# Three pairs of modulation chunks loaded and multiplied at the second mixer's entry, with other router, gather and gate rows

## The reference

```python
def moe(h, router_w, router_b, w_up, b_up, w_down, b_down):
    logits = (xt @ router_w + router_b).astype(jnp.float32)
    top_vals, top_idx = lax.top_k(logits, TOP_K)
    gates = jax.nn.softmax(top_vals, axis=-1)
    ...  # each token's four experts: swiglu(x @ w_up[e] + b_up[e]) @ w_down[e] + b_down[e]
    contrib = y_slots[dest] * gate_sorted[:, None]
...
def second_block(x, c, ...):
    c_act = jax.nn.silu(c)
    for l in range(DEPTH):
        mod = c_act @ w_ada[l] + b_ada[l]
        sh1, sc1, g1, sh2, sc2, g2 = jnp.split(mod[:, None, :], 6, axis=-1)
        h = ada_norm(x, norm1_g[l], sh1, sc1)      # rms_norm(x, g) * (1 + scale) + shift
        proj = h @ w_in[l]
        ...  # neighbourhood attention, latent attention, short convolution, group norm: mixed
        x = x + g1 * (mixed @ w_out[l])
        h2 = ada_norm(x, norm2_g[l], sh2, sc2)
        gt, up = jnp.split(h2 @ w_gu[l], 2, axis=-1)
        x = x + g2 * ((jax.nn.silu(gt) * up) @ w_down[l])
```

## Time and profile before

| | us |
|---|---|
| median of three runs | 1532.1 (1530.83 to 1532.83) |
| profiled execution, own time | 1531.5 |
| its span, first to last instruction | 1529.6 |
| first mixer ends, branches begin | 201.2 |
| first expert product | 267.8 |
| second mixer begins | 1184.2 |
| TensorE busy | 1423.6 (93%) |
| VectorE, ScalarE, GpSimd busy | 591.9, 444.9, 39.1 |

### The profile page before, as it was taken

One profiled execution on the slowest core, in us unless ns is written; L12 is line 12 of the kernel. 1 busy time (PEld: TensorE's weight loads), 2 busy tenths in 40 slices (PEclk: granted clock), 3 DMA queues, 4 the chain that ended last, 5 costly groups with the idle time before them and its releaser, 6 DMA issues. The chain is left out here.

```text
span 1529.6 us, 19821 instructions
## 1 busy us (share of the span) xinstructions
PE 1423.6 (93%) x7981; PEld 838.8 (55%) x7981; DVE 591.9 (39%) x1030; ACT 444.9 (29%) x577; POOL 39.1 (3%) x80
## 2 busy tenths in 40 slices
PE   8999999999999999988988988989988999899998
PEld 8988798344334434323423423323333788788887
DVE  4985447211210211210210210210211786677765
ACT  5654533121111112111111111111111536454343
POOL 2000030000000000000000000000000022000000
PEclk9999999999999999999999999999999999999999
DMA  9598999899999999999999999999999361345552
GB/s 283 171 299 272 327 334 397 361 426 429 427 428 428 428 428 428 429 428 428 429 428 429 428 429 428 429 428 429 428 427 382 104 191 56 99 150 193 192 187 88
DMA packets 126901, 516.46 MB, mean 338 GB/s; under 512 B 6869, under 2 KB 95294, under 8 KB 102238
## 3 DMA queue, kind: packets, MB, share of 16 engines
q1 hardware_dynamic: 126558, 514.64, 84.6%
q10 hardware_dynamic: 288, 1.05, 0.2%
HBM read 514.62 MB, written 1.05 MB: 337 GB/s over the span
## 5 line engine op out<-in xcount | busy, mean ns | idle before, releaser
L1307 PE MATMUL ps<-ring,xg 128*64 128x512 f32 x1456 | 324.8, 595 | 27.3 <-DMA ring<-in_expert_w_up 23.2
L1450 DVE TENSOR_TENSOR glu<-ps,bupT 128x512 f32<-128x512 f32 x32 | 22.1, 692 | 717.5 <-PE ps L1316 717.5
L1307 PEld LDWEIGHTS ps<-ring,xg 128*64 128x64 f32 x1456 | 101.7, 137 | 244.8 <-issue 186.2
L86 ACT ACTIVATE hrow<-ps 128x1024 f32<-128x1024 f32 x32 | 32.7, 1023 | 474.4 <-PE ps L1307 474.4
L1332 PE MATMUL ps<-ring,act 128*64 128x512 f32 x608 | 136.8, 597 | 1.2 <-ACT y L86 1.1
L2134 PE MATMUL ps<-h_halves,w_hi 128*128 128x512 f32 x352 | 123.1, 394 | 1.1 <-DVE h_halves L2287 1.1
L2236 DVE TENSOR_TENSOR w_lo<-ring,w_hi 128x2048 fp32r<-128x2048 f32 x36 | 82.5, 2291 | 61.2 <-ACT w_hi L86 61.2
L1307 PE MATMUL ps<-more,xg 128*64 128x512 f32 x416 | 93.1, 595 | 8.4 <-DMA more<-in_expert_w_up 7.2
L2136 PE MATMUL ps<-h_halves,w_lo 128*128 128x256 f32 x352 | 98.7, 280 | 0.0
L86 ACT ACTIVATE y<-ps 64x512 f32<-64x512 f32 x64 | 37.8, 591 | 182.8 <-PE ps L1332 182.5
L86 ACT ACTIVATE w_hi<-ring 128x2048 fp32r<-128x2048 f32 (+1 forms) x38 | 70.7, 1864 | 60.0 <-PE ps L2136 32.6
(11 more groups left out here) (409 smaller groups left out, 2218.1 us busy)
## 6 DMA issues: line engine op xcount, KB each, us to landing
ring<-in_expert_w_up SPq DMA_DIRECT2D x91, 2048.0 KB, 36.8
ring<-in_expert_w_down SPq DMA_DIRECT2D x38, 2048.0 KB, 39.3
more<-in_expert_w_up SPq DMA_DIRECT2D x26, 2048.0 KB, 35.5
more<-in_expert_w_down SPq DMA_DIRECT2D x16, 2048.0 KB, 38.8
ring<-in_w_in SPq DMA_DIRECT2D x29, 1024.0 KB, 9.0
ring<-in_w_ada SPq DMA_DIRECT2D x24, 1024.0 KB, 6.5
x_xT_xn<-in_expert_w_up SPq DMA_DIRECT2D x11, 2048.0 KB, 36.9
ring<-in_w_gu SPq DMA_DIRECT2D x22, 1024.0 KB, 5.1
```

The lines of the kernel that those rows point to most:

```text
L86: return nc.scalar.activation(out, x, ACT.Copy)
L1307: last = nc.tensor.matmul(up[a2 * CAP:(a2 + 1) * CAP, u, :], k.xg[:, q, h * CAP:(h + 1) * CAP], w[:, c:c + 512], start=(q == 0), stop=(q = ...
L1450: link(nc.vector.tensor_tensor(k.glu[:, :, :, :], g, b[:, 0].to_broadcast(wide), ALU.add))
```

## The change

- Modulation pairs 7, 8 and 9 (shift and scale of the second norm, SHIFT2 and SCALE2, and the rows between, which nothing needs before the output block) leave the first mixer. The other nine run after chunks 6, 8, 9, 11, 12, 14, 15, 17 and 18.
- SyncE loads their six chunks at the end of the experts into ring slots 4, 5, 6, 2, 3 and 1, after w_in_2 chunk 0 and before chunks 1 to 4.
- TensorE multiplies them at the second mixer's entry, two pairs before the transposes and one behind, in place of `fill`; the sums are copied by ScalarE, turned by TensorE after projection 1, added to `k.mod` by VectorE, and GpSimd makes the second norm's scale from them.
- `PLACE_SLOT` has the slots of places 1 and 2 exchanged.
- The router: the second token tile's transposes go to two banks each, ScalarE copies one half and VectorE the other; logits are computed in pairs of tiles; the top four are found by replacing them in a copy and comparing; the place counts from 1, so a subtraction goes; the ungated `choose` is one compare instead of four.
- The gather is done in halves with a copy each; of the first expert pair's, four of eight tiles stand before the block's barrier.
- The gate row g1 is multiplied in two pieces between the logits; g2 is multiplied at the output block's entry and copied there.

```diff
-PLACE_SLOT = {0: 6, 1: 0, 2: 2, 3: 8, 4: 10, 6: 4}
+PLACE_SLOT = {0: 6, 1: 2, 2: 0, 3: 8, 4: 10, 6: 4}
...
-ADA_FROM = 8
+ADA_LATE = (7, 8, 9)
+ADA_AT = dict(zip((6, 8, 9, 11, 12, 14, 15, 17, 18), (a for a in range(N_ADA) if a not in ADA_LATE)))
+ADA_ORDER = list(ADA_AT.values())
+LATE_SLOTS = ((4, 5), (2, 6), (1, 3))
...
-        pair = i - 1 - ADA_FROM
-        if 0 <= pair < N_ADA:
+        pair = ADA_AT.get(i - 1)
+        if pair is not None:
             two = [("ada", 2 * pair), ("ada", 2 * pair + 1)]
             out += two if len(out) % RING1 < RING1 - 1 else two[::-1]
...
+    ada_products(nc, k, 7, k.cwin, pair, slots, pair == ADA_ORDER[0], pair == ADA_ORDER[-1])
+
+
+def ada_products(nc, k, bank, cwin, pair, slots, first, last_pair):
...
     w = k.ring[:, slots[0]:slots[1] + 1:slots[1] - slots[0], :].rearrange("p s (k n) -> p s k n", k=KD)
     for q in range(KD):
         g = 32 * (q % 4)
-        last = nc.tensor.matmul(k.ps[g:g + 32, 7, :].rearrange("p (s n) -> p s n", s=2),
-                                k.cwin[:, q, 31 - pair:63 - pair], w[:, :, q, :], start=(pair == 0 and q < 4),
-                                stop=(pair == N_ADA - 1 and q >= 4), skip_group_check=True)
+        last = nc.tensor.matmul(k.ps[g:g + 32, bank, :].rearrange("p (s n) -> p s n", s=2),
+                                cwin[:, q, 31 - pair:63 - pair], w[:, :, q, :], start=(first and q < 4),
+                                stop=(last_pair and q >= 4), skip_group_check=True)
     last.then_inc(k.ada_step, 1)
...
+    if not gated:
+        both = [P, TT, 2, CAP]
+        return nc.vector.tensor_tensor(k.sel.rearrange("p t (h n) -> p t h n", h=2),
+                                       k.slots[:, :].unsqueeze(1).unsqueeze(1).to_broadcast(both),
+                                       k.place[:, :, bass.ds(p * 2, 2)].unsqueeze(3).to_broadcast(both), ALU.is_equal)
...
-                    last = nc.tensor.transpose(k.ps[:, bank[t][half], j * P:(j + 1) * P],
+                    b, at = (bank[t][half], j) if t == 0 else (bank[t][half] + 4 * (j // 2), j % 2)
+                    last = nc.tensor.transpose(k.ps[:, b, at * P:(at + 1) * P],
...
-            def logits(t):
-                for half in range(2):
-                    if (t, half) == (1, 1):
-                        pe.wait_ge(hT_last, 1)
+            def logits(t, pairs):
+                for n in pairs:
+                    if t == 0:
+                        pe.wait_ge(hT_ready, n // 2 + 1)
                     else:
-                        pe.wait_ge(hT_ready, 2 * t + half + 1)
-                    for q in range(4 * half, 4 * half + 4):
+                        pe.wait_ge((hT_ready, hT_last)[n % 2], (3, 1)[n % 2] + n // 2)
+                    for q in (2 * n, 2 * n + 1):
                         last = nc.tensor.matmul(k.ps[:, 4 + t, 0:E], hT[:, q, t * P:(t + 1) * P], k.rw[:, q, :],
                                                 start=(q == 0), stop=(q == KD - 1))
...
+                return last
...
+            def gate_row(half):
+                return nc.tensor.matmul(k.ps[:, half, :], k.ones[:, :], k.diag[0][:, half * 512:(half + 1) * 512],
+                                        start=True, stop=True)
...
-            logits(0)
-            gate_rows(0)
+            logits(0, range(4)).then_inc(log_done, 1)
+            gate_row(0)
             turn(1, 0)
+            logits(1, (0,))
             turn(1, 1)
-            logits(1)
-            gate_rows(1)
+            logits(1, (1, 2, 3)).then_inc(log_done, 1)
+            gate_row(1).then_inc(gb_done, 1)
             pe.wait_ge(m_ready, 2)
...
-            fill(nc, k, 3, k.h[:, 0, 0:512], 1)
+            pe.wait_ge(k.hot_ready, 1)
+            gather(nc, k, 5, range(4)).then_inc(k.g_done, 1)
 
...
-                link(nc.vector.tensor_tensor(lg[:, t, :], k.ps[:, 4 + t, 0:E], k.rb[:, :], ALU.add))
+                link(nc.vector.tensor_tensor(lg[:, t, 0:E], k.ps[:, 4 + t, 0:E], k.rb[:, :], ALU.add))
                 link(nc.vector.max(m8[:, t, :], lg[:, t, :]))
-                nc.vector.tensor_scalar(k.small[:, t:t + 1], m8[:, t, 0:1], -1.0, None, ALU.mult).then_inc(negmax, 1)
-                link(nc.vector.max_index(ix[:, t, :], m8[:, t, :], lg[:, t, :]))
-                link(nc.vector.tensor_copy(ixf[:, t, :], ix[:, t, :]))
-                link(nc.vector.tensor_tensor(one_hot[:, t], bc(k.iota[:, 0:E], 1, 4), bc(ixf[:, t, 0:4], 2, E), ALU.is_equal))
-                nc.vector.tensor_reduce(k.chosen[:, t, :], one_hot[:, t].rearrange("p j e -> p e j"), AX.X, ALU.add)\
+                link(nc.vector.match_replace(rest_lg[:, t, :], m8[:, t, :], lg[:, t, :], -LARGE))
+                nc.vector.tensor_tensor(k.chosen[:, t, :], rest_lg[:, t, 0:E], lg[:, t, 0:E], ALU.not_equal)\
                     .then_inc(m_ready, 1)
+                nc.vector.tensor_scalar(k.small[:, t:t + 1], m8[:, t, 4:5], -1.0, None, ALU.mult).then_inc(negmax, 1)
 
...
-            for i, slot in enumerate(LATE):
+            def load_slot(i):
                 src, kt, cols = k.last[i]
-                sp.wait_ge(used, done + slot_free(slot))
+                sp.wait_ge(used, done + slot_free(LATE[i]))
                 sp.dma_start(slot_last(k, i, kt, cols), src).then_inc(k.last_in[i], 16)
+
+            load_slot(0)
+            for n, (pair, slots) in enumerate(zip(ADA_LATE, LATE_SLOTS)):
+                for c, slot in sorted(enumerate(slots), key=lambda x: slot_free(x[1])):
+                    sp.wait_ge(used, done + slot_free(slot))
+                    sp.dma_start(k.ring[:, slot, :].rearrange("p (k n) -> p k n", k=KD), k.ada_chunks[2 * pair + c])\
+                        .then_inc(k.first_in[n], 16)
+            for i in range(1, len(LATE)):
+                load_slot(i)
 
...
-            pe.wait_ge(hot_ready, 1)
-            gather(nc, k, 5, range(KD)).then_inc(g_done, 1)
+            gather(nc, k, 5, range(4, KD)).then_inc(g_done, 1)
             extra = extra_rounds(pe)
             pe.wait_ge(k.bias_in, 32)
             def up_weights(r, turn, at, n, h):
                 for q in range(KD):
+                    if h == 0 and q % 4 == 0:
+                        pe.wait_ge(xg_ready, n * 2 + q // 4 + 1)
                     if q % 2 == 0:
                         chunk = expert_arrived(k, pe, r, turn, at * PAIR + h * UP_CHUNKS + q // 2)
...
-            act.wait_ge(g_done, 1)
-            act_copy(nc, k.xg[:, :, :].rearrange("p k n -> p (k n)"), flat(rows)).then_inc(xg_ready, 1)
+            def gathered(n, src):
+                for half in range(2):
+                    act.wait_ge(g_done, n * 2 + half + 1)
+                    act_copy(nc, k.xg[:, 4 * half:4 * half + 4, :].rearrange("p k n -> p (k n)"), src[:, half, :])\
+                        .then_inc(xg_ready, 1)
+
+            gathered(0, rows)
...
+            def late_rows(n):
+                pe.wait_ge(k.first_in[n], 16 * (FIRST_LOADS[n] + 2))
+                ada_products(nc, k, 3, k.late_cwin, ADA_LATE[n], LATE_SLOTS[n], n == 0, n == len(ADA_LATE) - 1)
+
             pe.wait_ge(k.bm_in, 16 * len(k.bm_loads))
             for b in range(4):
-                nc.tensor.matmul(k.ps[:, b, :], k.flip[:, :], bias_window(k, b // 2, b % 2),
+                nc.tensor.matmul(k.ps[:, 4 + b, :], k.flip[:, :], bias_window(k, b // 2, b % 2),
                                  start=True, stop=True).then_inc(bm_done, 1)
-            fill(nc, k, 4, k.gB[:, 0, 0:512], 5)
-            for t in range(TT):
+            pe.wait_ge(k.ada_copied, 2)
+            for n in range(2):
+                late_rows(n)
+            for t in range(TT):
+                pe.wait_ge(bm_out, t + 1)
                 pe.wait_ge(xn_ready, t + 1)
                 for m in range(KD):
                     last = nc.tensor.transpose(k.flat[:, 2048 + t * D + m * P:2048 + t * D + (m + 1) * P],
                                                xn[:, t, m * P:(m + 1) * P], k.ident[:, :])
                 last.then_inc(xnT_done, 1)
-            pe.wait_ge(bm_out, 2)
-            fill(nc, k, 3, k.gB[:, 0, 0:512], 2)
-            pe.wait_ge(hT_ready, 3 + 2 * TT)
+            late_rows(2)
+            pe.wait_ge(hT_ready, 4 + 2 * TT)
             projection(0)
             for i in range(1, 4):
                 split_projection(i)
+                if i == 1:
+                    ada_turn(nc, k, pe, 3, k.late_acc, 7)
             half_projection(4, 0)
             pe.wait_ge(ck_n, 1)
             transpose_tokens(nc, k, k.flat[:, 2048:3328], proj[:, :, 768:1408], 0, 5).then_inc(ck_t, 1)
...
+            act.wait_ge(k.ada_step, N_ADA)
+            act_copy(nc, k.late_acc, k.ps[:, 3, :]).then_inc(k.ada_copied, 1)
...
+            dve.wait_ge(k.ada_summed, 2)
+            a0 = ADA_LATE[0]
+            v = k.mod[:, 4 * a0:4 * (a0 + len(ADA_LATE))].rearrange("p (a m) -> p m a", m=4)
+            nc.vector.tensor_tensor(v, v, k.ps[:, 7, 0:P].rearrange("p (m a) -> p m a", m=4)[:, :, a0:a0 + len(ADA_LATE)],
```

(20 more changed lines are left out.)

121 lines of the change are left out of this document (63 added, 58 removed).

## The result

The changed kernel takes 1552.6 us (median of 4 runs, 1551.95 to 1553.21) against 1532.5 (1530.83 to 1533.4), a ratio of 1.0129, 95% interval 1.0115 to 1.0143. It is slower, as forecast, but by 20.1 us and not 11.9, and 1552.6 lies outside the range of 1536 to 1549.

What follows compares the result with a forecast made beforehand. TensorE was taken to bound the first mixer and transfers the experts, with SyncE last at the barrier. 1531.5 - 7.3 - 0.1 + 18.0 + 0.1 + 0.8 + 1.0 = 1544.0 us, range 1536 to 1549.

Steps and rivals of the forecast that it cites:

- First mixer: TensorE-bound first mixer: nine modulation pairs instead of twelve and shorter waits save 7.3 us (bounds -5.0 to -8.9).
- I take 0.5 us of it: First mixer: 0.5 us saved of TensorE's 1.4 us wait for VectorE, bounds -1.0 and +1.4.
- a pair now runs one place earlier, which gives it time: First mixer: an earlier pair gives VectorE time, though TensorE's earlier arrival could keep or lengthen its 1.4 us wait.
- Router and bias: Experts' start: token tiles some 2 us earlier, but the down-projection bias transfer hides it; -0.1 us, bounds 0 and -2.0.
- The clock at the barrier: Behind the experts' barrier: a slower pace after TensorE idles some 18 us, +1.0 us, bounds 0 and +3.7.
- End of the experts: SyncE's six added w_ada chunks, 3.0 us each and uncovered, hold the barrier: +18.0 us, bounds +15 and +19.
- Second mixer: Second mixer: third pair's products in place of a fill +0.1 us, turn of the sums among dense projections +0.8 us.
- The rivals: Six chunks hidden (1525, 8 in 100); mixer transfer-held (1533.3, 5); router's 2 us real (1542, 10); costlier restart (1547, 12).
- The third: Router's 2 us are real because the bias lands earlier or is not waited for: 1542 us, 10 in 100.

Runs made afterwards that it cites:

- p_place: Changed kernel with its nine first-mixer pairs behind chunks 8 to 16 instead of 6 to 18: 1550.8 us, ratio 1.0116.
- p_router: The change without its modulation part (all twelve pairs in the first mixer; new router, gather and gate rows): 1535.9 us, ratio 1.0022.
- p_after_pad: Changed kernel with an unused 64-byte tile ahead of x_hi and x_lo, putting them 32 beyond a multiple of 256: 1550.7 us, ratio 1.0115.
- p_router_bias: The change without its modulation part, with TensorE's wait for the down biases moved to the first scatter: 1533.8 us, ratio 1.0000.
- p_warm20: Changed kernel with nineteen unread products behind TensorE's last scatter of the experts: 1551.0 us, ratio 1.0115.
- p_warm: Changed kernel with forty unread products behind TensorE's last scatter of the experts: 1565.7 us, ratio 1.0220.
- p_fill: Changed kernel with four unread products in TensorE's wait at the seventh recurrence step: 1548.3 us, ratio 1.0105.
- p_before_pad: Kernel before, with an unused tile that moves x_hi and x_lo: 1535.6 us, ratio 1.0009.
- p_dose: Changed kernel loading three of the six late w_ada chunks at the end of the experts: 1542.1 us, ratio 1.0049.
- p_order: Changed kernel with the five w_in_2 chunks issued first and the six w_ada chunks behind them: 1551.2 us, ratio 1.0112.
- p_all: Changed kernel with pairs behind chunks 8 to 16, bias wait at first scatter, unread products in the eighth step's wait and the experts' end: 1561.7 us.
- p_sum: Changed kernel with pairs behind chunks 8 to 16, the 64-byte tile, and the down-bias wait at the first scatter: 1543.4 us, ratio 1.0057.
- p_best_pad: The change without its modulation part, bias wait at first scatter, one unread product in the eighth step's wait, 64-byte tile: 1530.9 us, ratio 0.9977.

## Why the prediction was wrong, and where it was right

*First mixer: "I take 0.5 us of it", in all -7.3 us (bounds -5.0 to -8.9).* This step failed; it was -1.9, so 5.4 us were missing. The sum took the remaining products to run at their old pace and the waits to cost only their own length. Neither held.

- The clock behind the longer wait. The step "a pair now runs one place earlier, which gives it time" had it the wrong way round: the pair put behind chunk 6 starts the recurrence's steps 2.6 us later (64.8 against 62.3), VectorE is busy without a break from 100 to 110 and cannot make it up, while TensorE, with no pair behind chunk 10, does. Hence the wait of 2.06 us where 0.3 had been; `p_place` removes it. The clock fell behind it: the mixer ended at 199.4 to 200.4 in the five kernels with that order and address in which the clock fell, at 197.2 and 197.6 in the two in which it did not, 2.3 us on the mean. With the clock up, the wait by itself shows no cost (197.45 without it, in `p_place`).
- The address of `x_hi` and `x_lo`, which the forecast put at nothing. The pace of the products changed in both directions with it and is 2.9 us of TensorE's time. How much of that reaches the mixer's end is less sure: `p_router` against the kernel before, the clock up in both, shows 1.3 us, and the 2.9 of `p_after_pad` hold some clock.

Together these are 3.6 to 5.2 of the 5.4 us.

*Router and bias: -0.1 (bounds 0 and -2.0).* That the bias hides the router's gain was right, and `p_router_bias` shows the size. The bound of 0 failed, for the same reason as above: a hidden gain is not free if what hides it is idle time on TensorE. The wait grew from 1.5 to 3.0 us, and the first 24 products behind it took 7.1 us instead of 5.4. Where the clock stayed up behind that wait, in `p_place` and `p_warm20`, the first refill came 70.8 and 70.5 us behind the branches' start, as before (70.4).

*The clock at the barrier: +1.0 (bounds 0 and +3.7).* It measured 1.25 (15.18 against 13.93 in `p_warm`), but that is one execution: in the nine kernels whose clock was low when this barrier opened it was 0.1 (`p_fill`) to 1.25. I applied the rule at the one place where TensorE would stand idle for 18 us, and not at the two where the change lengthened a short wait. The Trainium skill, page "TensorE: Matmul & The Clock Gate", section Part 1: The HAM clock gate, states that the clock is set by how busy TensorE has been recently. This trace agrees, by the granted clock of the three windows above. That no row of the kernel before showed a fall was in part luck: `p_before_pad`, the same instructions with a wait of 1.36 us at the eighth step, shows one.

*End of the experts: +18.0.* Right, with its reason: +17.9, 3.0 us a chunk in `p_dose`, by amount and not by order (`p_order`).

*Second mixer: +0.1 and +0.8.* Right (+0.3 by `p_warm`, +0.9).

The rivals: none occurred. The third (the router's 2 us are real) came true only where the wait was moved. That the change is slower, as forecast, rests on the 18 us of the six chunks alone.

What is left open: why the clock fell in some executions and not in others at the same wait, what of an operand's address makes a product slower (only four positions were tried), and what holds the last 0.2 to 1.8 us of the first mixer's miss.

## What to carry to other kernels

Where loads are moved from a stage bound by TensorE behind a stream that is full, each costs its whole transfer, whatever it replaces: here six chunks bought three pairs' 5.6 us for 18. When a change takes work off TensorE ahead of a wait, price the wait twice, once as idle time and once as the clock behind it (here the idle time was absorbed and the clock was not); and a gain hidden by another wait should be taken together with that wait, or not at all. Two unchanged stretches whose products differ by a few ns are worth a look at the addresses that new tiles have shifted.

## What the runs showed of the hardware

- The granted clock can fall behind short waits of a busy TensorE, and not each time. Behind 1.3 to 1.4 us at the eighth recurrence step it fell in 3 of 9 profiled executions, behind 2.1 to 2.5 us at the seventh in 6 of 8, behind 2.6 to 4.1 us at the experts' start in 7 of 9. Where both steps waited 0.6 us or less it fell there in none of 5, and in none of 8 behind a wait of 1.0 to 1.3 us for a transfer at 185 to 188 us. In four (`p_all`, `p_sum`, `p_dose`, `p_best_pad`) it fell in the router's stretch, at 253 to 257 us, among short products with waits of 0.5 us; 13 others have the same stretch without a fall. It reads 0.50 for 3.4 to 6.8 us then, and cost 1.7 us (the first 24 expert products) and 2.3 us (the mixer's end).
- Products of 256 columns from `x_hi` and `x_lo` start 117.1, 117.1, 118.7 and 119.8 ns apart with these at 0, 32, 96 and 224 bytes beyond a multiple of 256.
- SyncE's issue of a chunk in 1 KB rows ends when the chunk three places ahead has landed (in the changed kernel the last issue ended at 1202.75, and that chunk's last piece landed at 1202.90), and an all-engine barrier waits for it.
